# State-space stage: the running sums turned to rows once, and spread over the partitions by a float32r product per head

## The reference, cut to what matters

```python
a_cs = jnp.cumsum(dt * A, axis=2)                 # per chunk: 128 running sums for each head
seg = a_cs[:, :, :, None, :] - a_cs[:, :, None, :, :]
Lmat = jnp.exp(jnp.where(mask, seg, -jnp.inf))    # 128 x 128 decays for each head
scores = jnp.einsum('bclhn,bcshn->bclsh', Cm, Bm) * Lmat
y_diag = jnp.einsum('bclsh,bcshp->bclhp', scores, xdt)
states = jnp.einsum('bclhn,bclh,bclhp->bchpn', Bm, decay_to_end, xdt)
# carry = chunk_decay * carry + states ;  y_off = (C @ carry) * exp(a_cs)
```

## Time and profile before

| | us |
|---|---|
| runs, median (lowest to highest) of 3 | 3383.99 (3383.26 to 3387.25) |
| the profiled execution | 3382.88 |
| its span in the trace | 3381.0 |
| state-space stage with its start, first to last instruction (L980 to L1236) | 1569.2 to 1830.8 |
| start of one chunk's last sum of y (L1236) to the next, mean of 12 | 12.65 |

### The profile page before, as it was taken

The page is one execution under the profiler, slowest core; times in us unless marked ns, Lnnn a source line. Parts: engine busy times, 40 slices in busy tenths (PEclk is TensorE's granted clock), DMA queues, the critical chain, the costliest instruction groups (busy, mean ns, idle before and its releaser), DMA issues. The chain is left out here.

```text
span 3381.0 us, 42729 instructions
## 1 busy us (share of the span) xinstructions
PE 2945.9 (87%) x13075; PEld 2018.1 (60%) x13075; DVE 2321.7 (69%) x2858; ACT 1548.7 (46%) x1962; POOL 633.3 (19%) x421
## 2 busy tenths in 40 slices
PE   6999999669999999996997499958999999999960
PEld 3776776434444444443664277746788778778750
DVE  2555555437787787784776644457888888888869
ACT  2323323103333333335553233306877777787753
POOL 0000000000000000001894000012333334433335
PEclk8999999659999999998997699978999999999985
DMA  6112111553311111100003433347788896689738
GB/s 251 51 47 65 52 44 59 156 152 88 93 22 37 34 22 37 34 16 7 1 0 118 148 123 123 123 154 243 237 268 270 296 350 215 218 284 313 229 95 309
DMA packets 237898, 455.07 MB, mean 135 GB/s; under 512 B 19345, under 2 KB 93165, under 8 KB 237069
## 3 DMA queue, kind: packets, MB, share of 16 engines
q1 hardware_dynamic: 222421, 398.19, 34.8%
q0 software_dynamic: 15408, 56.11, 6.8%
q10 hardware_dynamic: 8, 0.01, 0.0%
HBM read 358.01 MB, written 96.25 MB: 134 GB/s over the span
## 5 line engine op out<-in xcount | busy, mean ns | idle before, releaser
L2202 DVE TENSOR_TENSOR weights_rest<-w,weights_rounded 128x2048 fp32r<-128x2048 f32 x315 | 716.3, 2288 | 115.6 <-ACT weights_rounded L2132 107.3
L2132 ACT ACTIVATE weights_rounded<-w 128x2048 fp32r x315 | 602.5, 1916 | 146.2 <-PE ps_up L2054 79.5
L845 ACT ACTIVATE probs<-ps_scores 128x1024 f32<-128x1024 f32 x260 | 266.0, 1023 | 505.0 <-PE ps_scores L776 428.8
L868 DVE TENSOR_REDUCE part_max<-ps_max 128x1 f32<-128x512 f32 (+1 forms) x528 | 337.9, 678 | 195.0 <-PE ps_max L753 194.9
L425 PE MATMUL ps_proj<-w_in,n1T 128*128 128x512 f32 (+2 forms) x1152 | 349.1, 461 | 6.5 <-PEq L108 6.5
L2054 PE MATMUL ps_up<-weights_rounded,block_T_rounded 128*128 128x512 f32 x832 | 336.9, 405 | 11.9 <-DVE block_T_rest L2210 11.9
L2054 PE MATMUL ps_up<-weights_rounded,block_T_rest 128*128 128x512 f32 x832 | 327.8, 394 | 0.0
L2054 PE MATMUL ps_up<-weights_rest,block_T_rounded 128*128 128x512 f32 x832 | 326.4, 392 | 0.0
L425 PEld LDWEIGHTS ps_proj<-w_in,n1T 128*128 128x128 f32 x1152 | 197.8, 193 | 146.0 <-issue 131.1
L786 PE MATMUL ps_attn<-probs,v 128*64 128x512 f32 x1040 | 283.6, 625 | 0.0
L753 PE MATMUL ps_max<-kT,q_for_max 128*128 128x512 f32 (+1 forms) x528 | 191.4, 436 | 76.0 <-DVE part_max L868 41.5
(11 more groups left out here) (354 smaller groups left out, 4956.5 us busy)
## 6 DMA issues: line engine op xcount, KB each, us to landing
w<-in_w SPq DMA_DIRECT2D x96, 2048.0 KB, 12.4
w_ada_rest<-in_w_ada SPq DMA_DIRECT2D x5, 2048.0 KB, 15.5
scratch_y<-zero_rows SPq DMA_DIRECT2D x19, 512.0 KB, 5.5
scratch_qT<-qT_stage SPq DMA_DIRECT2D x18, 512.0 KB, 3.5
q_for_max<-scratch_qT SPq DMA_DIRECT2D x36, 256.0 KB, 5.8
q_rounded_twice<-scratch_qT SPq DMA_DIRECT2D x36, 256.0 KB, 4.4
mix_rows<-scratch_mix SPq DMA_DIRECT2D x18, 512.0 KB, 5.1
scratch_h<-h_rows SPq DMA_DIRECT2D x18, 512.0 KB, 2.6
```

Source lines behind the costliest of these rows:

```text
L845: act.activation(pf[:, slot(p, n), :], ps_s[:, n % 2, :], ACT.Exp).then_inc(exp_done, 1)
L868: nc.vector.tensor_reduce(mx[:, p, n // H, n % H:n % H + 1], ps_m[:, n % 2, 0:PART], AX.X, ALU.max).then_inc(m_taken, 1)
L2132: act.activation(split_piece(wh, s), raw_piece(s, buf[0]), ACT.Copy).then_inc(hi_done, 1)
L2202: nc.vector.tensor_tensor(split_piece(wl, s), raw_piece(s, buf), split_piece(wh, s).bitcast(F32), ALU.subtract).then_inc(lo_done, 1)
```

## The change

The sums are no longer made diagonal in every chunk. Once, ahead of the loop, VectorE writes them as columns in two parts, the value rounded to float32r (`tensor_copy` to a float32r view) and the rest, into a tile `acs_cols` that lies in the space of `decays` and was zeroed by POOL. PE transposes each of the 18 chunks' 128 columns (18 instructions, into three PSUM areas), and VectorE copies them out as `acs_rows` (two of 128 x 1,024 and one of 128 x 256). ScalarE waits for these copies (`stats_ready` 4) before it copies the first chunk. Per chunk, `copy_chunk` copies one chunk's rows to `acs_chunk` in float32r (one more ACTIVATE, 128 x 128). `spread` then first adds the mask (two float32r products of 512 columns, as before) and then makes eight float32r products of 128 columns, one a head: `chosen` holds for each head a matrix with ones in the two rows of that head, so the product puts that head's sums on every partition. `chosen` is made by POOL ahead of the loop (two 128 x 1,024 additions). POOL's `diag_sums` goes away, and in its list `split_c(c + 2)` stands ahead of `scale_x(c + 1)`.

```diff
         @block.gpsimd
+            gp.memset(acs_cols, 0.0).then_inc(cleared, 1)
             gp.memset(carry[:, :, :], 0.0).then_inc(cleared, 1)
+            for d in range(2):
+                rounded, rest = (S["ident"][:, at:at + H].rearrange("p (h o) -> p h o", o=1).to_broadcast([P, H, P]) for at, heads in parts[d::2])
+                gp.tensor_tensor(chosen[:, d * H:(d + 1) * H, :], rounded, rest, ALU.add).then_inc(cleared, 1)
...
             split_c(0, 0)
-            diag_sums(0, 0)
-            diag_sums(0, 1)
             split_c(1, 1)
-            diag_sums(1, 0)
             scale_x(0, 0)
             for c, p in query_tiles(gp, NT):
                 if not (isinstance(c, int) and c == NT - 1):
-                    diag_sums(c + 1, 1)
-                    scale_x(c + 1, 1 - p)
                     if not (isinstance(c, int) and c == NT - 2):
                         split_c(c + 2, p)
-                        diag_sums(c + 2, 0)
+                    scale_x(c + 1, 1 - p)
...
-                act.activation(cc[:, p, :], cT[:, t], ACT.Copy).then_inc(xs_ready, 1)
+                act.activation(cc[:, p, :], cT[:, t], ACT.Copy)
+                wait_alone(act, bc_ready, c * 2 - 2, S["passed"])
+                act.activation(acs_chunk[:, p, :].rearrange("p (o n) -> p o n", o=1), acs_rows[:, bass.ds(c, 1), :], ACT.Copy).then_inc(xs_ready, 1)
...
+            act.wait_ge(stats_ready, 4)
             copy_chunk(0, 0)
...
+            pe.wait_ge(cols_split, 2)
+            for c in range(NT):
+                bank, at = divmod(c % 8, 4)
+                cols = slice(at * P, (at + 1) * P)
+                out = b_a[:, c * P:(c + 1) * P] if c < 8 else b_s[:, bank, cols] if c < 16 else b_o[:, cols]
+                last = nc.tensor.transpose(out, acs_cols[:, c, :], S["ident"][:, :])
+            last.then_inc(sums_ready, 1)
...
-                pe.wait_ge(sacs_ready, c * 2 + d + 1)
+                pe.wait_ge(xs_ready, c + 1)
                 wait(pe, e_ready, c * 2 + d)
...
-                    nc.tensor.matmul(b_a[:, n * 512:(n + 1) * 512], masks[:, 2, :], sacs[:, d * H + n * 4:d * H + n * 4 + 4, :],
-                                     start=True, stop=False)
-                for n in range(2):
-                    last = nc.tensor.matmul(b_a[:, n * 512:(n + 1) * 512], identr[:, :], bars, start=False, stop=True)
+                    nc.tensor.matmul(b_a[:, n * 512:(n + 1) * 512], identr[:, :], bars, start=True, stop=False, skip_group_check=True)
+                for h in range(H):
+                    last = nc.tensor.matmul(b_a[:, h * P:(h + 1) * P], chosen[:, d * H + h, :], acs_chunk[:, p, :],
+                                            start=False, stop=(h % 4 == 3), skip_group_check=True)
...
+            dve.wait_ge(cleared, 1)
+            for at, heads in parts[:2]:
+                last = nc.vector.tensor_copy(acs_cols[:, :, at:at + H].bitcast(F32R), stats[:, :, ACS, heads])
...
+                last = nc.vector.tensor_tensor(acs_cols[:, :, at:at + H], stats[:, :, ACS, heads], acs_cols[:, :, rounded:rounded + H], ALU.subtract)
...
+            dve.wait_ge(sums_ready, 4)
+            for c0, src in ((0, b_a[:, :]), (8, b_s[:, :, :].rearrange("p b n -> p (b n)")), (16, b_o[:, 0:2 * P])):
+                n = src.shape[1] // P
+                nc.vector.tensor_copy(acs_rows[:, c0:c0 + n, :].rearrange("p c n -> p (c n)"), src).then_inc(stats_ready, 1)
```

More of the change, by code:

```diff
@@ L953, in ssm_phase @@
         cbd = sb("chunk_C_blocks", [P, 2, SSM_G, P])
-        sacs = sb("diag_sums", [P, N2, P])
+        acs_rows = sb("sum_rows", [P, NT, P])
+        chosen = sb("row_selectors", [P, N2, P], F32R)
+        acs_chunk = sb("chunk_sum_rows", [P, 2, P], F32R)
         sm = sb("chunk_stats", [P, 2, 6, N2])
@@ L959, in ssm_phase @@
         e = sb("decays", [P, 2, 2, H, P])
+        acs_cols = e[:, :, :, :, :].rearrange("p a d h n -> p (a d h n)")[:, 0:NT * P].rearrange("p (c n) -> p c n", n=P)
+        parts = [(u * HD + d * 32, slice(d * H, (d + 1) * H)) for u in range(2) for d in range(2)]
         xd = sb("scaled_x", [P, 2, 5, W])
@@ L971, in ssm_phase @@
         prep_a, prep_d, sums_ready, stats_ready, cleared = sem("prep_act"), sem("prep_dve"), sem("sums_ready"), sem("stats_ready"), sem("cleared")
-        xs_ready, sacs_ready, sm_ready, turned, xt_ready, cbd_ready = (sem(n) for n in ("xs_ready", "sacs_ready", "sm_ready", "turned", "xt_ready", "cbd_ready"))
+        xs_ready, sm_ready, turned, xt_ready, cbd_ready = (sem(n) for n in ("xs_ready", "sm_ready", "turned", "xt_ready", "cbd_ready"))
         bc_ready, e_ready, g_ready, xd_ready, barred_ready = (sem(n) for n in ("bc_ready", "e_ready", "g_ready", "xd_ready", "barred_ready"))
@@ L975, in ssm_phase @@
             sem(n) for n in ("st_ready", "yof_ready", "yd_ready", "carry_ready", "stb_ready", "y_ready", "dve_own"))
+        cols_split = sem("sum_cols_split")
         block = ctx.enter_context(nc.Block())
@@ L990, in split_c @@
                                         ALU.mult).then_inc(cbd_ready, 1)
[L992 to L998, removed]
             def scale_x(c, p):
@@ L1111, in turn, with spread @@
                 nc.tensor.matmul(b_c[:, P:3 * P], xs[:, p, 4, :], cbd[:, p, :, :], start=True, stop=True).then_inc(turned, 1)
-            def spread(c, d):
-                pe.wait_ge(sacs_ready, c * 2 + d + 1)
+            def spread(c, p, d):
+                pe.wait_ge(xs_ready, c + 1)
                 wait(pe, e_ready, c * 2 + d)
@@ L1147, in _ @@
             pe.wait_ge(barred_ready, 2)
-            spread(0, 0)
-            spread(0, 1)
+            pe.wait_ge(cleared, 4)
+            spread(0, 0, 0)
+            spread(0, 0, 1)
             for c, p in query_tiles(pe, NT):
@@ L1153, in _ @@
                     turn(c + 1, 1 - p)
-                    spread(c + 1, 0)
+                    spread(c + 1, 1 - p, 0)
                 states(c, p)
@@ L1158, in _ @@
                 if more:
-                    spread(c + 1, 1)
+                    spread(c + 1, 1 - p, 1)
                 inside(c, p, 1)
@@ L1190, in _ @@
             own.link(nc.vector.tensor_tensor(w1, w4, stats[:, :, ACS, :], ALU.subtract))
+            dve.wait_ge(cleared, 1)
+            for at, heads in parts[:2]:
+                last = nc.vector.tensor_copy(acs_cols[:, :, at:at + H].bitcast(F32R), stats[:, :, ACS, heads])
+            last.then_inc(cols_split, 1)
+            dve.wait_ge(cols_split, 1)
+            for (at, heads), (rounded, _) in zip(parts[2:], parts[:2]):
+                last = nc.vector.tensor_tensor(acs_cols[:, :, at:at + H], stats[:, :, ACS, heads], acs_cols[:, :, rounded:rounded + H], ALU.subtract)
+            last.then_inc(cols_split, 1)
             dve.wait_ge(prep_a, 5)
@@ L1198, in _ @@
             last.then_inc(stats_ready, 1)
+            dve.wait_ge(sums_ready, 4)
+            for c0, src in ((0, b_a[:, :]), (8, b_s[:, :, :].rearrange("p b n -> p (b n)")), (16, b_o[:, 0:2 * P])):
+                n = src.shape[1] // P
+                nc.vector.tensor_copy(acs_rows[:, c0:c0 + n, :].rearrange("p c n -> p (c n)"), src).then_inc(stats_ready, 1)
             dve.wait_ge(stats_ready, 1)
-            dve.wait_ge(cleared, 1)
+            dve.wait_ge(cleared, 2)
             loop = Tally(dve, dve_own)
```

## The result

The changed kernel took 3338.14 us (median of 4 runs, 3336.68 to 3340.35), the kernel before 3383.62 beside it: a ratio of 0.986, 95% interval 0.985 to 0.988. On a second chip it took 3341.41 against 3383.06, 0.988 (0.987 to 0.990).

A forecast was written before the change was run, and what follows sets the result against it. A two-chunk circle through POOL and PE bounds the kernel; 16 chunks falling from 12.71 to 10.6 give -33.7 us, the start +1.5: profiled 3382.88 becomes 3350.7, median 3352. Forecast's range 3343 to 3358; 8 in 10, 3343 to 3374.

The forecast's parts named there:

- POOL leaves the limiting circle; PE no longer waits for it: Chunk loop: POOL loses two instructions, 4.73 us a chunk, and C's blocks' 0.6 us leaves the path to PE.
- A spread at 1.34, 0.11 a head product: PE's spread: two mask products and eight head products at 0.11 take 1.34 us, before 2.24 to 2.3.
- A (0.23): Rival on PE's spread: a 128-column float32r product costs 0.23, as one of 512; 3372 us, chance 18%.
- B (0.43): Rival on PE's spread: a head product costs 0.43, like an old float32 spread instruction; 3424 us, chance 7%.
- The circle through ACT and DVE, 8.81 without w: Chunk loop: the circle left, 6.21 to the second exponentials' end plus 2.60 after the mask product; 10.56 with w.
- w: Time of VectorE's second mask product in a chunk, taken as 1.75 us, bounds 1.23 and 2.27.
- Rival C: DVE's mask product never gets past POOL: w stays 2.49, a chunk is 11.3; 3363 us, chance 20%.
- The tail: After the first exponentials of chunk 17 (1810.56): the same work, so no change in time.
- The start, +1.5: Stage start to chunk 1's first exponentials: new copies and slow first turn add 1.5 us, bounds 0 and 4.0.
- PE waits 0.9 us a chunk: Chunk loop: PE's list is 9.7 us against a chunk of 10.6, so PE waits 0.9, about as before.
- What the order is worth: POOL's list: with C's blocks ahead of the scaling, their 0.6 us leaves the path from scaled copies to PE.

The follow-up runs named there:

- the third kernel: The changed kernel with POOL still making the diagonal sums at their old places, read by nobody: 3371.70 us, ratio 0.9969 to the kernel before.
- The earlier spread: The changed kernel with two moves on ACT and PE's second spread two heads earlier: 3338.19 us, ratio 0.9871 to the kernel before.
- the sixth copy: The changed kernel with one more scaled copy of x a chunk on POOL, unread: 3349.34 us, ratio 0.9904 to the kernel before.

## Why the prediction was off, step by step

- **POOL leaves the limiting circle; PE no longer waits for it:** right. POOL is idle 2.21 a chunk. Leaving the sums in costs 2.1 a chunk in the third kernel's profile, its slowest run, part of it at half clock; by the ratios of the medians the whole kernel is 29 to 36 us slower than the changed one.
- **A spread at 1.34, 0.11 a head product:** right. The second spread of a chunk takes 1.39 (1691.01 to 1692.40), the first 0.1 more, at 0.105 a product, 0.11 by doubling. Rivals A (0.23) and B (0.43) are out. The rule of the Trainium skill that the prediction cites ("TensorE: Matmul & The Clock Gate", Part 3, What overlaps and what doesn't: a load overlaps a running product only on other rows) would have given 0.16; neither measurement bears it out.
- **The circle through ACT and DVE, 8.81 without w:** right. 6.22 + 2.57 = 8.79.
- **w, taken as 1.75 between 1.23 and 2.27: the step that failed.** It is 1.23 in all but one chunk of the loop (1.62). Of the 0.58 by which the steady chunk is below 10.6, w is 0.52. Over 16 chunks 0.58 is 9.3; the first two chunks, 11.55 and 10.55, take 2.1 of it back, and the loop came out 7.3 below the forecast. The place was right (POOL at its last copy or at the blocks when DVE asks), but I took a middle for want of an account of what decides: the meeting falls at the same point of every turn, here 0.11 before POOL's copy ends. Rival C had seen that it recurs and put it on the wrong side. The earlier spread and the sixth copy show how near that is: with 0.27 us more of POOL's copy left it is 1.46, with 0.83 more 2.02. Also, the line of mask products in the earlier trace rows mixes two kinds: its 2.07 in the middle is the first one of each chunk, before and after; the second, which is w, had taken 2.39 to 2.53 in the steady loop before. So C's "half of these products take 2.07 or more" says little of w.
- **The tail, "the same work", 0:** the second step that failed, -4.2. The work is the same; its clock is not (2.8), and the second exponentials start 1.4 sooner. With w at 1.23 alone the time is at the low end of the range, 3343, which was reckoned so; the tail is the largest of the terms that lead beyond it. It was put at nothing without a look at the clock there. Why the clock stays up now is open, as said under the experiments.
- **The start, +1.5:** +0.6; a size. The first exponentials of chunk 0 come 30.2 after the stage's first instruction, for 29.6 forecast.
- **PE waits 0.9 us a chunk:** wrong, 0.1 to 0.2, since w is shorter and PE's list is 9.84, not 9.7 (10.02 less 0.19: from the states to the product with the carry, which waits for y, there are 1.91, 1696.46 to 1698.37, where it was 1.72).
- **What the order is worth:** I priced it as 0.6 us of POOL that leave a path. For the kernel before this was about right. For the changed kernel it guards 1.9 a chunk in the one execution that was traced, the slowest of seven; I neither priced that in the prediction nor, by size, in the experiment's expectation.

Of the profiled execution: 3350.7 forecast, less 7.3 in the loop, 4.2 in the tail, 0.9 in the start and 1.5 ahead of the stage, and 3.6 more behind it, is 3340.4; it took 3340.35.

## What to carry to other kernels

When two engines hinder each other in a loop that repeats, the cost is not a mean between the ends: it is set by where in the turn they meet. Forecast when the second one asks and how much of the other's instruction is left then, and give both ends a chance of their own; here 0.11 us left cost nothing, 0.38 cost 0.23 and 0.94 cost 0.79. When two engines are near their limit, price a change to both together: apart these were worth 1.0 and 0.35 (at most about 0.8) us a chunk, together 2.4. And "the same work" at a stage's end is the same time only if the waits ahead of it, and so perhaps the clock, stay the same.

## What was not expected of the hardware

A product on POOL beside one of DVE's can be lengthened as much as the other way round: the blocks took 1.64 instead of 0.61, a copy 2.02 instead of 1.04. The Trainium skill ("SBUF — State Buffer", Who interferes with whom), which says that the first to issue blocks the other, agrees with both. And one wait of PE of 2.40 us, in the old order, cost 1.6 us more by the half clock that followed it (3.87 instead of 2.29 to the states).
